# Latent attention: query rows for the rotation made once and moved by transfers, key rows moved on SyncE's queue

## The reference

```python
proj = h @ w_in                                   # 1024 -> 384 + 256 + 32
c_q, c_kv, k_rope = proj[..., :384], proj[..., 384:640], proj[..., 640:]
q  = (rmsnorm(c_q, q_norm) @ w_uq).reshape(B, S, 16, 64 + 32)
kv = (rmsnorm(c_kv, kv_norm) @ w_ukv).reshape(B, S, 16, 64 + 64)
q_nope = q[..., :64]
q_rope = apply_rotary(q[..., 64:], cos, sin)      # pairs 16 + 16: x1 cos - x2 sin, x1 sin + x2 cos
k_rope = apply_rotary(k_rope, cos, sin)           # one for all heads
s = (q_nope . k_nope + q_rope . k_rope) * 96 ** -0.5
p = softmax(where(kpos <= qpos, s, NEG)); o = p @ v; o @ w_o
```

## Time and profile before

| | us |
|---|---|
| median of 3 runs | 1406.79 |
| lowest, highest | 1406.29, 1407.12 |
| the profiled execution | 1407.12 |
| its span in the profile | 1405.3 |
| TensorE busy | 1392.9 (99% of the span) |
| VectorE busy | 915.3 (65%) |
| ScalarE busy | 740.8 (53%) |
| GpSimd busy | 73.9 (5%) |

### The profile page before, as it was taken

How to read it: one execution, slowest core, us unless ns; L and a number is a source line. 1 busy time by engine, 2 the same in 40 slices (tenths; PEclk the granted TensorE clock), 3 DMA queues, 4 the chain that set the end, 5 groups by cost and what they waited for, 6 DMA issues and landing times.

```text
span 1405.3 us, 21648 instructions
## 1 busy us (share of the span) xinstructions
PE 1392.9 (99%) x8384; PEld 1237.7 (88%) x8384; DVE 915.3 (65%) x1170; ACT 740.8 (53%) x913; POOL 73.9 (5%) x113
## 2 busy tenths in 40 slices
PE   9999999999999999999999999999999999999997
PEld 8989989988888888899888888888889999888886
DVE  5555787675566666677666666756567676665656
ACT  6656673344355444557554444544445558554444
POOL 2000010010020000010120000000000002200000
PEclk9999999999999999999999999999999999999999
DMA  8534441255535555462375554655545410555552
GB/s 312 205 141 149 153 149 61 91 195 195 193 133 204 201 184 191 168 206 80 126 268 197 193 201 174 244 188 203 181 179 184 156 51 2 204 200 183 198 185 90
DMA packets 34767, 239.60 MB, mean 170 GB/s; under 512 B 3914, under 2 KB 4058, under 8 KB 6928
## 3 DMA queue, kind: packets, MB, share of 16 engines
q1 hardware_dynamic: 32832, 231.39, 46.2%
q0 software_dynamic: 1440, 6.67, 1.4%
q10 hardware_dynamic: 432, 0.66, 0.1%
HBM read 237.10 MB, written 1.08 MB: 169 GB/s over the span
## 4 chain that ended last, share of the span: by engine, by line
PE 95%; ACT 2%; DVE 2%; issue 1%; POOL 0%; POOLq 0%; ACTq 0%; DVEq 0%
PE ps L737 22%; PE ps L707 15%; PE ps L709 15%; PE ps L708 15%; PE ps L745 11%; PE ps L1038 3%; PE ps L1012 2%; PE ps L1022 1%; PE ps L1360 1%; PE ps L2949 1%; PE ps L2957 1%; PE ps L646 1%; PE ps L2961 1%; PE ps L3127 1%; PE ps L828 1%
## 5 line engine op out<-in xcount | busy, mean ns | idle before, releaser
L413 DVE TENSOR_TENSOR low<-raw,high 128x2048 fp32r<-128x2048 f32 (+1 forms) x212 | 481.3, 2272 | 231.3 <-ACT high L407 228.7
L407 ACT ACTIVATE high<-raw 128x2048 fp32r<-128x2048 f32 (+1 forms) x215 | 406.5, 1893 | 75.7 <-PE ps L709 71.4
L737 PE MATMUL ps<-nt,high 128*128 128x512 f32 x1344 | 320.1, 390 | 0.0
L737 PEld LDWEIGHTS ps<-nt,high 128*128 128x128 f32 x1344 | 249.0, 188 | 49.8
L745 PEld LDWEIGHTS ps<-nt,low 128*128 128x128 f32 x1344 | 167.5, 189 | 3.6
L745 PE MATMUL ps<-nt,low 128*128 128x256 f32 x1344 | 168.6, 283 | 0.0
L707 PE MATMUL ps<-high,hth 128*128 128x512 f32 x320 | 124.5, 389 | 0.0
L708 PE MATMUL ps<-low,hth 128*128 128x512 f32 x320 | 124.5, 389 | 0.0
L709 PE MATMUL ps<-high,htl 128*128 128x512 f32 x320 | 124.5, 389 | 0.0
L707 PE MATMUL ps<-nt,high 128*128 128x256 f32 x400 | 114.3, 286 | 0.0
L709 PE MATMUL ps<-nt,low 128*128 128x256 f32 x400 | 113.3, 283 | 0.0
(11 more groups left out here) (425 smaller groups left out, 2076.0 us busy)
## 6 DMA issues: line engine op xcount, KB each, us to landing
raw<-in_stream SPq DMA_DIRECT2D x215, 1024.0 KB, 4.8
late<-in_w POOLq DMA_DIRECT2D x1, 2048.0 KB, 9.4
scr<-bias_by_distance POOLq DMA_DIRECT2D x1, 2048.0 KB, 14.9
scr<-in_mem SPq DMA_DIRECT2D x2, 512.0 KB, 5.0
raw<-in_stream SPq DMA_DIRECT2D x4, 256.0 KB, 6.6
raw<-in_stream SPq DMA_DIRECT2D x2, 512.0 KB, 7.7
x<-in_x SPq DMA_DIRECT2D x1, 1024.0 KB, 8.5
con<-in_con SPq DMA_DIRECT2D x1, 592.0 KB, 8.9
```

Of the source, the lines that this page charges most:

```text
L407: nc.scalar.activation(high_of(t, slice(0, n)), raw[t % SLOTS][:, 0:n], ACT.Copy).then_inc(w_high, 1)
L413: nc.vector.tensor_tensor(low_of(t, slice(0, n)), raw[t % SLOTS][:, 0:n], high_of(t, slice(0, n)).bitcast(F32), ALU.subtract).then_inc(w_l ...
L737: last = nc.tensor.matmul(r3(bank, 2), w[:, k, P * j:P * j + P], nt[:, :, k, :], start=first and k == 0, stop=not first and k == KC - 1, s ...
```

## The change

The weights of the queries are laid out anew. `uq0` now holds the 32 rope rows of all 16 heads (512 columns: 16 heads x x1, x2), `uq1` and `uq2` the 64 rows without position, two heads in a bank of 128 rows. `uq3` is gone, and all tiles behind it move up by one.

- VectorE multiplies the two banks of `uq0` by a table of cos and by a table of sin, 128 x 512 four times (L2602 of the changed kernel), into `ml_turned`. There is no addition of the two parts: rows 64 to 95 of `mq` get the part with cos and rows 96 to 127 the part with sin, and the keys get two groups of 32 rows that give the same sum in the scores (x1 cos - x2 sin and the like come out of a product over 128 rows in place of 96). The key's rope rows take two multiplications, a subtraction and an addition.
- ScalarE and VectorE each copy half of the rows of `uq1` and `uq2`.
- SyncE issues, behind the load of `uv`, one transfer for the key rows (64 partitions x 16 heads x 256) and then, after a wait for `ml_qd`, eight for the query rows (32 partitions x 4 heads x 256 each). All loads of the stream from `mlao0` on stand behind them in its list. GpSimd's transfer of the key rows (32 partitions x 16 x 256) is gone.
- The input root is spread alone, right behind the first half of `uq0` and all the sums; the key-value root stays behind `uq1`. ScalarE copies the first spread root (`ml_spread` 1) before it splits `uq2`.
- ScalarE rounds the key-value latents ahead of its split of `uv`, and VectorE takes their rest ahead of its.
- Tables: `before` (128 columns, not used) and `rope` (256) go, `cos` and `sin` (256 each) come, so that `con` grows by 128 columns. `poss` moves into `small`.

```diff
-    q = np.concatenate([q, q[:, :, 80:96], q[:, :, 64:80]], axis=2).reshape(MLA_QL, MLA_H * P)
-    for j in range(4):
-        put(f"uq{j}", cols(q, 512 * j, 512))
+    nope, rope = (np.ascontiguousarray(v).reshape(MLA_QL, -1) for v in (q[:, :, :MLA_N], q[:, :, MLA_N:]))
+    put("uq0", cols(rope, 0, 512))
+    for j in range(2):
+        put(f"uq{j + 1}", cols(nope, 512 * j, 512))
...
-            UNITS.append(dict(products=[(r3(ml["q"], MLA_H)[0:96, h, :], r3(ml["k"], MLA_H)[0:96, h, :])],
+            UNITS.append(dict(products=[(r3(ml["q"], MLA_H)[:, h, :], r3(ml["k"], MLA_H)[:, h, :])],
...
+            def sp_latent_rows(sp):
+                sp.wait_ge(ml_kr, 1)
+                sp.dma_start(mk_[64:128, :, :], rep(mlc["kr"][64:128, S:2 * S], MLA_H)).then_inc(ml_krd, 16)
+                sp.wait_ge(ml_qd, 2)
+                for j in range(4):
+                    for n in range(2):
+                        sp.dma_start(mq[64 + 32 * n:96 + 32 * n, j::4, :], ml_turned[n][32 * j:32 * j + 32])\
+                            .then_inc(ml_qrd, 16)
+            for t in range(SLOTS * latent, SLOTS * latent + SLOTS):
+                sp_tile(sp, t)
+                if t == TILE["uv"]:
+                    sp_latent_rows(sp)
...
-            pool.wait_ge(ml_kr, 1)
-            pool.dma_start(mk_[64:96, :, :], rep(mlc["kr"][64:96, S:2 * S], MLA_H)).then_inc(ml_krd, 16)
...
-            for j in range(4):
-                act_step(act, f"uq{j}")
+            act.wait_ge(ml_spread, 1)
+            nc.scalar.activation(m_rows[64:128, 0:S], ps[7][64:128, 0:S], ACT.Copy).then_inc(ml_rows, 1)
+            act_step(act, "uq0")
+            for j in (1, 2):
                 if j == 2:
                     act.wait_ge(ml_kvm, 1)
                     nc.scalar.activation(ch_[:, 3:5, :], m_kvn, ACT.Copy).then_inc(ml_kvhigh, 1)
+                act_step(act, f"uq{j}")
...
-                if j == 1:
-                    pe.wait_ge(ml_diag, 4)
-                    for n in range(4):
+                    if j == b and j < 2:
+                        pe.wait_ge(ml_diag, TT * j + TT)
+                        for n in range(TT * j, TT * j + TT):
                             last = nc.tensor.matmul(pair(ps[7], n), ones, m_diag[:, n, :], start=True, stop=True)
-                    last.then_inc(ml_spread, 1)
+                        last.then_inc(ml_spread, 1)
...
+            pe.wait_ge(ml_qrd, 16 * 8)
```

More of the change, by code:

```diff
@@ L62, in plan @@
     t += ffn_names(0)
-    t += ["mlain0", "mlain1", "mlain2"] + [f"uq{j}" for j in range(4)] + ["uk", "uv"]
+    t += ["mlain0", "mlain1", "mlain2"] + [f"uq{j}" for j in range(3)] + ["uk", "uv"]
     t += [f"mlao{j}" for j in range(4)]
@@ L84 @@
 GATE_AND_UP = {f"f{f}{part}{i}" for f in range(4) for part in "gu" for i in range(FT)}
-USED = {"ba": KC * P, "ng": KC * P, "uq0": 1536, "uq1": 1536, "uq2": 1536, "uq3": 1536}
+USED = {"ba": KC * P, "ng": KC * P, "uq0": 1536, "uq1": 1536, "uq2": 1536}
 TILE = {n: i for i, n in enumerate(PLAN)}
@@ L110 @@
 _at = 0
-for _n, _w in (("ident", 128), ("gains", 128), ("upto", 128), ("before", 128), ("ones", 128), ("causal", 256),
-               ("window", 256), ("rope", 256), ("rowok", 32)):
+for _n, _w in (("ident", 128), ("gains", 128), ("upto", 128), ("ones", 128), ("causal", 256),
+               ("window", 256), ("cos", 256), ("sin", 256), ("rowok", 32)):
     CON[_n] = _at
@@ L137, in constants @@
     ang = np.arange(S, dtype=np.float32)[None, :] * inv[:, None].astype(np.float32)
[L139 to L142, removed]
+    put("cos", np.tile(np.cos(ang), (8, 1)))
+    put("sin", np.tile(np.concatenate([np.sin(ang), -np.sin(ang)]), (4, 1)))
     level = np.zeros((P, LEVELS, P), np.float32)
@@ L326, in c_ @@
             return con[:, CON[name]:CON[name] + w]
-        ident, upto, before, ones = (c_(n, P) for n in ("ident", "upto", "before", "ones"))
+        ident, upto, ones = (c_(n, P) for n in ("ident", "upto", "ones"))
         causal, window = c_("causal", 256), c_("window", 256)
@@ L1824, in _, with sp_tiles, sp_tile @@
                     sp.dma_start(row[:], A["row"]).then_inc(row_here, 16)
[L1825 to L1833, removed]
+            def sp_tiles(sp, first, end):
+                with sp.Fori(first, end) as i:
+                    for c in range(SLOTS):
+                        tile = sp.snap(i * SLOTS + c)
+                        sp.wait_ge(w_low, i * SLOTS + (c - SLOTS + 1))
+                        sp.dma_start(raw[c][:], A["stream"][bass.ds(tile, 1)].rearrange("o p w -> (o p) w"))\
+                            .then_inc(raw_here[c], 16)
+            def sp_tile(sp, t):
+                sp.wait_ge(w_low, t - SLOTS + 1)
+                sp.dma_start(raw[t % SLOTS][:], A["stream"][t]).then_inc(raw_here[t % SLOTS], 16)
+            def sp_latent_rows(sp):
[6 more added lines that the diff above has]
+                            .then_inc(ml_qrd, 16)
+            latent = TILE["uv"] // SLOTS
+            sp_tiles(sp, 2, latent)
+            for t in range(SLOTS * latent, SLOTS * latent + SLOTS):
+                sp_tile(sp, t)
+                if t == TILE["uv"]:
+                    sp_latent_rows(sp)
+            sp_tiles(sp, latent + 1, NT // SLOTS)
+            for t in range(NT // SLOTS * SLOTS, NT):
+                sp_tile(sp, t)
             for t in range(TT):
@@ L2571, in _ @@
                         .then_inc(ml_kvlow, 1)
+                dve_step(dve, f"uq{j}")
                 for b in range(2):
                     uq_here(dve, j, b)
[L2574 to L2585, removed]
-                if j == 1:
[L2587 to L2592, removed]
+                    h = 8 * (j - 1) + 4 * b
+                    nc.vector.tensor_copy(mq[0:64, h + 1:h + 4:2, :], r3(ps[2 * (j % 2) + b][64:128, :], 2))\
+                        .then_inc(ml_qd, 1)
             for b in range(4):
@@ L3043, in _ @@
             C_ = (ch_, cl_)
-            for j in range(4):
+            for j in range(3):
                 t = TILE[f"uq{j}"]
```

95 lines of the change are left out of this document (57 added, 38 removed).

## The result

| | before | after |
|---|---|---|
| median of 9 executions each, us | 1406.79 | 1410.64 |
| lowest, highest | 1406.29, 1407.13 | 1410.23, 1411.25 |
| ratio after / before, 95% interval | | 1.0029 (1.0020 to 1.0037) |
| span of the profiled execution (its own time) | 1405.3 (1407.12) | 1408.9 (1410.72) |
| granted clock of TensorE, mean | 0.999 | 0.996 |

The changed kernel is slower, by 3.85 us. Three executions of the later series lasted far longer than all others (3835.07 us of e4, 7540.25 and 1521.45 of before beside e1 to e4 and e5 to e7) and are left out of ranges and ratios.

A forecast was written before the change was run, and what follows sets the result against it. TensorE, busy 99% of the span, was taken as the bound, with VectorE nearly as full there. -4.33 (tile) + 1.8 (VectorE's chain) + 5.0 (ScalarE behind the transfers) = +2.5 us, giving 1409.3; range 1404.0 to 1412.5.

The forecast's parts named there:

- VectorE idle until: VectorE's split of uq2 waits for ScalarE's: idle from about 614.6 to 618.6 us, then no pause.
- `mlao0` there: Load of mlao0, behind key and query rows on SyncE's queue, lands at 639.0 us; ScalarE wants it at about 631.7.
- the tile: TensorE's query stage: one tile of four goes, 36 products fewer, -4.33 us.
- VectorE's chain, wait before `uk`: Before uk: VectorE finishes the latents at 629.6 us, not 627.8, so 1.8 us of the saving are lost.
- ScalarE behind the transfers: Before the scores: ScalarE's key copies stand behind its split of the late mlao0, so TensorE waits, +5.0 us.
- the clock: TensorE's granted clock behind the pause before the scores: no cost in the forecast's sum, 0 us.
- rival (d): Behind the 5 us pause before the scores TensorE's clock falls to its lower level: +3, 1412.3 us, chance 0.16.
- The transfers' price: SyncE's queue: 6.8 us for the key rows and 6.0, a guess, for the query rows.
- (a): Transfers quick, at up to 3.9 us each; ScalarE in time, VectorE's chain decides: -2.5, 1404.3 us, chance 0.20.
- Rival (c): Ports' rate: 4.8 us for each of two transfers, scores start at 639.9: -0.7, 1406.1 us, chance 0.13.
- the eight issues: SyncE's issues of the query-row transfers: 0.33 us each, lasting until 626.7, hidden by the data in front.
- GpSimd's diagonals: GpSimd's root and diagonals, 1.01 and at most 2.34 us, done by 624.2, inside the same gap.

The follow-up runs named there:

- e4: Changed kernel with the key and value copies ahead of the split of mlao0 on ScalarE and VectorE, SyncE's order kept: 1404.61 us, ratio 0.9986.
- e1: Changed kernel with SyncE issuing the load of mlao0 ahead of the nine transfers of key and query rows: 1404.02 us, ratio 0.9982.
- e5: Changed kernel with both the mlao0 load ahead of the nine transfers and ScalarE's uq2 split ahead of its spread-root copy: 1401.77 us, ratio 0.9967.
- e7: Changed kernel with the key-row transfer reading the cos table on partitions 0 to 63 instead of key rows on 64 to 127: 1409.11 us, one execution.
- e2: Changed kernel with 20 unused TensorE products of 128 columns filling the pause before the scores: 1408.06 us, ratio 1.0011.
- e9: The kernel of e3 run once more, unchanged, for the profile of another execution: 1405.94 us.
- e3: Changed kernel with ScalarE splitting uq2 before it copies the spread input root: 1406.45 us, ratio 1.000.
- e10: The kernel of e3 with 14 unused products of 128 columns filling TensorE's pause before the scores: 1405.03 us, ratio 0.9988.
- e8: The kernel of e5 with the ten one-column sums made three times over, 30 in place of 10: 1409.47 us, ratio 1.0022.

## Why the prediction was right, and what it missed

The forecast was 1409.3 with a range of 1404.0 to 1412.5, and 1410.64 was measured. The direction, and the reason for it, held: a saved tile, a chain on VectorE, and a load behind nine transfers. Step by step, with 0.83 taken off the times for the earlier start of this execution:

| step | predicted | less 0.83 | measured |
|---|---|---|---|
| VectorE idle until | 618.6 | 617.8 | 617.99 |
| key rows ready (`ml_kr`) | 621.3 | 620.5 | 620.5 |
| query rows ready (`ml_qd` 2) | 624.0 | 623.2 | 623.1 |
| `uk` starts | 629.6 | 628.8 | 628.90 |
| TensorE ready for the scores | 638.1 | 637.3 | 637.5 |
| `mlao0` there | 639.0 | 638.2 | 637.8 |
| scores start | 643.1 | 642.3 | 641.76 |

| term of the sum | predicted | measured |
|---|---|---|
| the tile | -4.33 | -4.33 (e5: the scores 4.50 earlier) |
| VectorE's chain, wait before `uk` | +1.8 | +1.96 |
| ScalarE behind the transfers | +5.0 | +4.35 |
| the clock | 0 | +2.95 |
| earlier start; products at 1075 us | 0 | -0.83; -0.36 |
| sum | +2.5 | +3.7 |

- **That the number fitted was in part luck.** The four terms that belong to the change add up to +4.9 in this trace, twice the +2.5 of the forecast; the -0.83 and the -0.36, which vary with the execution and the series, bring that to +3.7.
- **The clock was the step that failed.** The sum made TensorE stand still for 5.0 us, three times the longest pause in the trace of before, and still priced the clock at nothing. The mechanism was rival (d), with a price of +3 that measured 2.95 in the trace and 2.1 to 2.6 by e2; only its chance, 0.16, was too low. A pause beyond anything that the trace has shown harmless should have carried its clock in the forecast itself: +5.5 and 1412.3, less the 0.65 by which the pause was shorter, less 1.2 for the two small items, is 1410.5. The Trainium skill (TensorE: Matmul & The Clock Gate, "HAM oscillation — how this bites in real kernels") says that waits for transfers take the clock down; after, e2 and e9 agree, with 0.50 behind pauses of 4.2 and 2.45 us that a late load caused, and the full clock behind a filled one.
- **The transfers' price was nearly exact.** Key rows 6.8 us (1.05 MB at 154 GB/s), as from the earlier trace rows; SyncE's queue carries them no faster than GpSimd's did. The query rows took 6.2 (628.1 to 634.3), where 6.0 was a guess. Its reason, that half of them are read from partitions which the writes don't touch, is borne out: those took 2.5 us at 220 GB/s, the others 3.7, and e7 shows the same for the key rows. That excluded (a), which needed 3.9 us each.
- **Rival (c)** gave each transfer 4.8 us; they took 6.8 and 6.2. The Trainium skill (SBUF — State Buffer, "Door 1: The DMA port swizzle") has twice the partitions in the upper half bring no more rate: after agrees, with 154 GB/s over 64 partitions against 153 over 32. Its 218 GB/s are reached when the source lies in the other half (220 in after, some 205 in e7) and missed when it does not.
- **Right by compensation:** the eight issues were priced at 0.33 us each and took 9.14 in all, 2.65 at most for one. The load of `mlao0` was thus issued at 632.28, not at 626.7. It cost little because the data in front ended about 634.3, but it did show: from 633.6 to 634.2 the transfer engines were busy for a third of the time. In e7, where the key rows were quicker, they were busy for 0.63 of the time from 632 to 634. So at the speed of (a) the issues, which I didn't name, would have been the limit at least in part, though they too were faster there (7.33 in e7). Two more sizes made up for each other: the first data moved 1.4 us after the issue (near 622.0) in place of 2.2, and `mlao0` landed 3.5 us after the data in front ended, in place of 2.6, while more than its own 1.05 MB moved (1.51 from 634.3 to 637.9, pieces of `mlao1` among them).
- **Wrong without effect:** GpSimd's diagonals took 0.73 us, not up to 2.34.

```profile
621.52 0.73 POOL L1914 TENSOR_SCALAR late<-con,small 128x128 f32<-128x128 f32 x2
```

Open: the cause of -0.36 at 1075 to 1105 us, and how often 10 sums take the clock down (in the profiled executions of e3 and e10 they did, in those of after, e1, e2, e4, e5, e7 and e9 not). One of the 19 executions of before in the series of e8 to e10 took 1411.47 at a mean clock of 0.994; it has no trace, so the clock can fall in the kernel before too, and where is not known. That small items tip the clock to one side or the other is possible and was not tried.

## What to carry to other kernels

The price of a moved transfer is what stands behind it: look up the next load on its queue, then the next instruction on the engine that uses that load, then who waits there. A tile that is fetched ahead of its use should be issued, and split, behind whatever the next stage needs and ahead of what nobody waits for: here two reorderings turned +3.9 into -4.7 us with the same work. If a forecast makes TensorE stand still for longer than any pause in the trace, put the clock's fall into the sum, and test it by filling the pause with idle products.

## What the runs showed of the hardware beyond that

- The granted clock also fell to 0.50 with TensorE busy all the time: behind 30 products of one column in every execution (e8), behind 10 in some (e3, e10). Behind a pause it fell after 4.22, 2.83 (e7) and 2.45 us (e9), and not after the 1.44 us of e3 and the 1.64 us before `uk` in after. "Busy 2.00 of 2.00" in the windows doesn't tell that the clock will stay.
- Copies within the core, written to partitions 64 to 127: 154 GB/s when they are read from the same half, some 205 to 220 from the other (after, e7).
- Issuing a transfer of 32 partitions x 4 heads x 256 costs SyncE 0.6 to 2.6 us (after), against 0.34 for a load of 1 MB with nothing in front and 0.59 for the one right behind them; the eight took 9.14 us while the transfers in front of them were moving.
- GpSimd's 128x128 scaling with a scalar took 0.73 us for two beside VectorE's reads out of banks, and 2.34 beside an instruction of VectorE with two operands on the core (L413).
